# Tokens loaded already turned in a hybrid decoder block

## The reference

```
h = rmsnorm(x, norm_mix_w[l])            # x * rsqrt(mean(x*x) + eps) * w
proj = h @ w_in[l]
q, k, v, g, a_low, z, xbc, dt_raw = jnp.split(proj, split_pts, axis=-1)
... gla_out from q, k, v, g, a_low; ssd_out from z, xbc, dt_raw
x = x + concatenate([gla_out, ssd_out]) @ w_out[l]
h2 = rmsnorm(x, norm_ffn_w[l])
x = x + moe_ffn(h2, ...)                 # top 4 of 32 experts
return rmsnorm(x, final_norm_w)
```

## Time and profile before

| | us |
|---|---|
| median of 3 runs | 3452.66 (3452.18 to 3453.17) |
| the profiled execution | 3451.21 |
| its span on the core | 3449.3 |
| TensorE busy | 3383.7, 98% of the span |
| VectorE, ScalarE, GpSimd busy | 2166.1, 1612.5, 628.4 |
| one round (from round 2 on) | 124.9 |

### The profile page before, as it was taken

One profiled execution on the slowest core, in us unless ns is written; L12 is line 12 of the kernel. 1 busy time (PEld: TensorE's weight loads), 2 busy tenths in 40 slices (PEclk: granted clock), 3 DMA queues, 4 the chain that ended last, 5 costly groups with the idle time before them and its releaser, 6 DMA issues.

```text
span 3449.3 us, 56541 instructions
## 1 busy us (share of the span) xinstructions
PE 3383.7 (98%) x21127; PEld 3075.8 (89%) x21127; DVE 2166.1 (63%) x2796; ACT 1612.5 (47%) x2079; POOL 628.4 (18%) x840
## 2 busy tenths in 40 slices
PE   7999999999999999999999999999999999999997
PEld 6778888888888999999999999988888888888986
DVE  4565455445556555555566666577777777777777
ACT  4433333233333444444444444455555555555555
POOL 1011111111114111111121112121112212212213
PEclk9999999999999999999999999999999999999998
DMA  9888888897866555666566666567667767777878
GB/s 385 345 345 296 308 302 295 305 326 273 290 251 199 173 171 166 184 179 179 179 192 195 186 192 205 181 209 243 208 206 225 245 210 230 245 228 224 250 244 316
DMA packets 475311, 826.54 MB, mean 240 GB/s; under 512 B 21853, under 2 KB 419325, under 8 KB 458816
## 3 DMA queue, kind: packets, MB, share of 16 engines
q1 hardware_dynamic: 443392, 721.84, 60.0%
q0 software_dynamic: 24320, 75.95, 9.6%
q10 hardware_dynamic: 7488, 27.27, 2.2%
HBM read 726.16 MB, written 98.96 MB: 239 GB/s over the span
## 4 chain that ended last, share of the span: by engine, by line
PE 94%; DMA 2%; ACT 1%; DVE 1%; POOL 1%; issue 1%; SPq 0%; POOLq 0%; DVEq 0%; ACTq 0%
PE acc L2474 15%; PE pp L2069 13%; PE acc L2470 11%; PE acc L2471 10%; PE acc L2472 10%; PE acc L2476 7%; PE acc L2486 4%; PE acc L2488 4%; PE acc L2487 4%; PE pp L2058 3%; PE tpm L2443 2%; PE pp L2059 2%; PE tp L2035 1%; PE tpm L2449 1%; DMA uraw<-in_w_in 1%; PE seg L2170 1%
## 5 line engine op out<-in xcount | busy, mean ns | idle before, releaser
L1891 DVE TENSOR_TENSOR wlo<-raw,whi 128x2048 fp32r<-128x2048 f32 x384 | 875.9, 2288 | 302.4 <-ACT whi L1281 302.3
L1281 ACT ACTIVATE whi<-raw 128x2048 fp32r<-128x2048 f32 x384 | 730.1, 1910 | 152.6 <-PE acc L2488 102.3
L2474 PE MATMUL acc<-xhl,whi 128*128 128x512 f32 (+3 forms) x2304 | 763.8, 385 | 0.0
L690 POOL TENSOR_TENSOR gate_op<-gate_op 1x1 f32<-1x1 f32 x348 | 175.2, 504 | 2714.4 <-DVE ybuf L1929 526.2
L2476 PE MATMUL acc<-xhl,wlo 128*128 128x256 f32 (+3 forms) x2304 | 624.3, 271 | 0.0
L2470 PE MATMUL acc<-xhl,whi 128*128 128x272 f32 (+3 forms) x1792 | 534.9, 298 | 1.2 <-DVE xhl L1903 1.2
L2471 PE MATMUL acc<-xhl,whi 128*128 128x272 f32 (+3 forms) x1792 | 530.3, 296 | 0.0
L2472 PE MATMUL acc<-xhl,wlo 128*128 128x272 f32 (+3 forms) x1792 | 530.2, 296 | 0.0
L2474 PEld LDWEIGHTS acc<-xhl,whi 128*128 128x128 f32 x2304 | 432.0, 187 | 68.4
L1314 ACT ACTIVATE work<-acc,bgu 128x256 f32<-128x256 f32 (+7 forms) x400 | 173.1, 470 | 584.6 <-PE acc L2472 366.2
L2476 PEld LDWEIGHTS acc<-xhl,wlo 128*128 128x128 f32 x2304 | 437.3, 190 | 0.7
(11 more groups left out here) (336 smaller groups left out, 5369.3 us busy)
## 6 DMA issues: line engine op xcount, KB each, us to landing
u<-split_d SPq DMA_DIRECT2D x112, 2048.0 KB, 9.2
raw<-in_moe_w_gate SPq DMA_DIRECT2D x128, 1024.0 KB, 5.2
raw<-in_moe_w_up SPq DMA_DIRECT2D x128, 1024.0 KB, 5.3
raw<-in_moe_w_down SPq DMA_DIRECT2D x128, 1024.0 KB, 9.3
split_d<-u SPq DMA_DIRECT2D x16, 2048.0 KB, 13.0
uraw<-in_w_in SPq DMA_DIRECT2D x12, 1024.0 KB, 11.0
yT<-in_moe_b_down SPq DMA_DIRECT2D x18, 512.0 KB
xin<-in_x ACTq DMA_DIRECT2D x14, 512.0 KB, 9.8
```

Source lines behind the costliest of these rows:

```text
L690: pool.tensor_tensor(gate_op[0:1, 0:1], gate_op[0:1, 1:2], gate_op[0:1, 1:2], ALU.add).then_inc(gate_ran, 1)
L1281: act.activation(whi[:, q % RING, :, :], raw[:, q % RING, :, :], ACT.Copy).then_inc(a_hi, 1)
L1891: dve.tensor_tensor(wlo[:, q % RING, :, :], raw[:, q % RING, :, :], whi[:, q % RING, :, :].bitcast(F32), ALU.subtract).then_inc(v_lo, 1)
L2474: pe.matmul(into[:, 0:2 * n].rearrange("p (c n) -> p c n", c=2), hi_, of[:, k, :, 0:n], start=(k == 0), stop=False)
```

## The change

The host lays out x a second time as `x_turned`, with the features on the partitions: for each pair 128 partitions of 8 x 256 numbers, 8 KB in one run, as `hraw` wants them. In rounds 1 to 6 ScalarE issues one load of 1 MB of it into `hraw`, as the first thing of its body. The scaling pass is left out for tiles 4 to 15, and instead of eight transposes TensorE makes one, of the column of 128 roots read over and over (`roots_spread`): the result has the roots of the tokens along the free axis, the same on each partition. VectorE then multiplies the loaded rows by the norm's weight and by this (`turned_rows`, eight operations of 128x128). x is still loaded into `xin` as well, for the squares. GpSimd makes a root only after the transpose of the one before has read `st`, and the load into `xin` waits for the former square, no longer for the former transposes.

```diff
+        def done_twice(inst, first, second):
+            s, i = where[first]
+            turn[s] += 2
+            inst.then_inc(S[s], 2)
...
-            def norm_root(j, n):
+            def norm_root(j, n, turned=False):
                 after(pool, "act_norm.sq", j)
+                if turned:
+                    after(pool, "pe_tx.tx", j - 1)
...
             def x_in(j):
-                after(act, "pe_tx.tx", j - 2 if isinstance(j, int) and j == 2 else j - 1)
+                if isinstance(j, int) and j <= 4:
+                    after(act, "pe_tx.tx", j - 2 if j == 2 else j - 1)
+                else:
+                    after(act, "act_norm.sq", j - 1)
                 act.dma_start(xin[:, :], x[0, bass.ds(j * P, P), :]).then_inc(d_x, 16)
...
+                turned = not (isinstance(j, int) and j < 4)
+                if turned:
+                    after(act, "p_norm.rstd", j - 1)
+                c = act.activation(junk[:, :], src, ACT.Square, scale=1.0 / 32.0, accum_out=st[:, 0:1])
+                if turned:
+                    done_twice(c, "act_norm.sq", "act_norm.xn")
...
+                if tx and at >= 1:
+                    after(act, "dve_h.lo", s)
+                    act.dma_start(hraw[:, :, :], x_turned[bass.ds(s + 1, 1)].rearrange("one p k i -> (one p) k i")).then_inc(d_xt, 16)
                 if post:
...
-                if tx:
+                if tx and at == 0:
                     norm_xn(a + 3)
...
-                if more:
-                    norm_xn(a + 4)
...
+            def turned_rows(s, t):
+                after(dve, "pe_tx.tx", s * 2 + 2 + t)
+                dve.wait_ge(d_xt, s * 16)
+                for k in range(KD):
+                    rows = hraw[:, k, t * P:(t + 1) * P]
+                    c = dve.scalar_tensor_tensor(out=rows, in0=rows, scalar=nw[:, k:k + 1], in1=tp[:, 0:P],
+                                                 op0=ALU.mult, op1=ALU.mult)
+                done(c, "dve_hT.hT")
...
-                    h_rows(a + 2, 0)
+                    h_rows(a + 2, 0) if at == 0 else turned_rows(s, 0)
...
-                    h_rows(a + 3, 1)
+                    h_rows(a + 3, 1) if at == 0 else turned_rows(s, 1)
...
+            def roots_spread():
+                done(pe.transpose(tp[:, 0:P], st[:, 1:2].to_broadcast([P, P]), ident[:, :]), "pe_tx.tx")
...
-                    after(pe, "act_norm.xn", a + 2)
+                    after(pe, "act_norm.xn" if at == 0 else "p_norm.rstd", a + 2)
...
-                    transposes(8, lambda c: xin[:, c * P:(c + 1) * P], "pe_tx.tx")
+                    if at == 0:
+                        transposes(8, lambda c: xin[:, c * P:(c + 1) * P], "pe_tx.tx")
+                    else:
+                        roots_spread()
...
+    x_turned = _np.asarray(inputs["x"][0]).reshape(PAIRS, PW, KD, P).transpose(0, 3, 2, 1)
```

More of the change, by code:

```diff
@@ L141, with build @@
 PRIMED = UNITS
-def build(nc, x, columns, shared, moe_cols, w_in, gla_w_alpha_up, w_out, router_w, moe_w_gate, moe_w_up, moe_w_down, moe_b_down, final_norm_w, out):
+def build(nc, x, x_turned, columns, shared, moe_cols, w_in, gla_w_alpha_up, w_out, router_w, moe_w_gate, moe_w_up, moe_w_down, moe_b_down, final_norm_w, out):
     with ExitStack() as ctx:
@@ L323, in done @@
             inst.then_inc(S[s], 1)
+        def done_twice(inst, first, second):
+            s, i = where[first]
+            assert turn[s] % len(STEPS[s]) == i and where[second] == (s, i + 1), (first, turn[s])
+            turn[s] += 2
+            inst.then_inc(S[s], 2)
         def after(eng, step, n):
@@ L334, in build @@
         d_ru = [sem(f"d_ru{s}") for s in range(4)]
-        v_ws = sem("v_ws")
         a_uh, v_ul, pe_un = sem("a_uh"), sem("v_ul"), sem("pe_un")
         d_un, d_st = ([sem(f"{n}{s}") for s in range(4)] for n in ("d_un", "d_st"))
-        d_x, d_x1 = sem("d_x"), sem("d_x1")
+        d_x, d_x1, d_xt = sem("d_x"), sem("d_x1"), sem("d_xt")
         d_xres, d_x2, d_h2 = ([sem(f"{n}{t}") for t in range(2)] for n in ("d_xres", "d_x2", "d_h2"))
@@ L759, in body @@
                 if tx:
-                    norm_root(s * 2 + 3, n)
+                    norm_root(s * 2 + 3, n, at >= 1)
                     n = n + 1
@@ L771, in body @@
                 if more:
-                    norm_root(s * 2 + 4, n)
+                    norm_root(s * 2 + 4, n, True)
                     n = n + 1
@@ L971, in norm_sq @@
                 src = xres[:, 1, :] if second else xin[:, :]
-                done(act.activation(junk[:, :], src, ACT.Square, scale=1.0 / 32.0, accum_out=st[:, 0:1]), "act_norm.sq")
+                turned = not (isinstance(j, int) and j < 4)
[5 more added lines that the diff above has]
+                else:
+                    done(c, "act_norm.sq")
             def norm_xn(j):
@@ L1751, in small_weights @@
                 dve.wait_ge(d_wsm, 32)
-                dve.tensor_copy(wsr[:, :, 0:SMALL], wsm[:, :, :]).then_inc(v_ws, 1)
-                dve.wait_ge(v_ws, 1)
+                dve.tensor_copy(wsr[:, :, 0:SMALL], wsm[:, :, :]).then_inc(setup_v, 1)
+                dve.wait_ge(setup_v, DVE_SETUP + 1)
                 dve.tensor_tensor(wsr[:, :, 64:SROWS], wsm[:, :, :], wsr[:, :, 0:SMALL].bitcast(F32),
-                                  ALU.subtract).then_inc(v_ws, 1)
+                                  ALU.subtract).then_inc(setup_v, 1)
             h_rows(0, 0)
@@ L2094, in small @@
                 if isinstance(s, int) and s == 0:
-                    pe.wait_ge(v_ws, 2)
+                    pe.wait_ge(setup_v, DVE_SETUP + 2)
                 for k in range(KD):
@@ L2276, in body @@
                 if tx:
-                    after(pe, "act_norm.xn", a + 3)
+                    after(pe, "act_norm.xn" if at == 0 else "p_norm.rstd", a + 3)
                     if post:
@@ L2582, in _ @@
             chunk(i, SIZES[-1], True)
-_INS = ["x", "columns", "shared", "moe_cols", "w_in", "gla_w_alpha_up", "w_out", "router_w", "moe_w_gate",
+_INS = ["x", "x_turned", "columns", "shared", "moe_cols", "w_in", "gla_w_alpha_up", "w_out", "router_w", "moe_w_gate",
         "moe_w_up", "moe_w_down", "moe_b_down", "final_norm_w"]
@@ L2602 @@
     moe_cols = biases.reshape(E * 3 * KD, P).T
-    inputs = {**inputs, "columns": columns, "shared": shared, "moe_cols": moe_cols}
+    x_turned = _np.asarray(inputs["x"][0]).reshape(PAIRS, PW, KD, P).transpose(0, 3, 2, 1)
+    inputs = {**inputs, "x_turned": x_turned, "columns": columns, "shared": shared, "moe_cols": moe_cols}
     nc = _bacc.Bacc("TRN2", target_bir_lowering=False, num_devices=1)
```

## The result

The changed kernel took 3496.92 us (median of 4 runs, 3488.86 to 3499.49), the kernel before 3452.42 us on the same chip (4 runs). The ratio is 1.0123, 95% interval 1.0111 to 1.0135: slower by 1.2%, where 3456 us and a range up to 3470 were forecast. The profiled execution took 3488.86 us, so its trace shows 37.7 us of loss against the 3451.21 us of before's; the median has some 8 us more, on which see the last point of "Why the prediction was wrong".

The account below looks back on a forecast made before the run. The prediction took TensorE's own queue to bound the rounds touched. Terms -9.1 - 0.5 + 12.0 + 0.9 = +3.3 us on 3452.7 gave 3456 us, own range 3446 to 3460, wider range 3443 to 3470.

Parts of the forecast that it names:

- The transposes: TensorE, tiles 4 to 15: seven transposes fewer save 0.76 us a tile, 9.1 us for twelve tiles.
- VectorE's 2.15 us: VectorE: eight small products with a PSUM operand take 2.2 us a tile, 0.9 us more than the two before.
- the load's landing: `hraw` load: issued at 496.5, landed by 505.5; VectorE waits about a us, hurting only beyond 507.
- the place of the stall: TensorE idles 2 to 3 us before `x_piece(s, 2)`, put down to VectorE's xT sum.
- the delay D of the writes: ScalarE's queue: both xacc_d writes come later behind the 1 MB load, by 4.5 us, range 1 to 7.3.
- rival (b): Writes come much later: load gains nothing by its lead, delay 7.3 us, total 3470 us; chance 0.30 together with another rival.
- the slack formula: `x_piece(s, 2)` start less `h2_of` start less 2.45, less 0.76 for TensorE's earlier arrival; delay beyond this slack stalls TensorE.
- The estimate of 4.4 us for the load: DMA: skill's gpsimd-path fit, 2.0 us plus bytes over 436 GB/s; would mean no stall; the prediction doubted it.
- nothing is as near: VectorE, second tile of a round: longer products cost nothing, as the PSUM bank's next user stands far behind in TensorE's queue.
- stall before `x_piece(s, 2)`: TensorE, five rounds: waits of 2.1, 2.0, 2.9, 1.7 and 3.3 us from late writes, 12.0 us together.
- `decays` waits for `ssd_add`: TensorE, round 1: the late load delays products and `ssd_add` before `decays`; 0.9 us, bounds 0 and 5.
- round 0: ScalarE: dropping the scaling pass before a copy TensorE waited for gains 0.5 us, bounds 0 and 0.5.

Follow-up runs that it names:

- e8: Changed kernel with the load issued early, `ssd_add` ahead of `turned_rows`, and weight unit 3 of rounds 2 to 6 held until both writes landed: 3445.77 us, 0.9975 to before.
- e2: Changed kernel with the load issued from SyncE's queue, ahead of weight unit 3, instead of ScalarE's: 3485.19 us, 1.0081 to before.
- e6: Changed kernel with weight unit 3 of rounds 2 to 6 held on SyncE until both xacc_d writes have landed: 3460.06 us, 1.0014 to before.
- e5: The repaired kernel: changed kernel with the load issued early and `ssd_add` ahead of `turned_rows` for both tiles: 3449.54 us, 0.9986 to before.
- e1: Changed kernel with the load issued at the end of the round before, ahead of `ssd_squares(a)`: 3458.64 us, 1.0016 to before.
- e9: Kernel before the change, with only weight unit 3 of rounds 2 to 6 held until both writes have landed: 3453.09 us, 1.0002 to before.
- e3: Changed kernel with the load issued behind both xacc_d writes on ScalarE's queue: 3540.13 us, 1.0244 to before.
- e7: Changed kernel with 40 unused identity products on TensorE ahead of the transposes of `h2` in rounds 2 to 6: 3517.09 us, 1.0184 to before.
- e11: Changed kernel with 18 unused identity products on TensorE ahead of the transposes of `h2`, to fill the gap: 3488.50 us, 1.0101 to before.

## Why the prediction was wrong

**What held.** The transposes: a round of the repaired kernel lasts 123.43 us against 124.93, 1.50 less, where 2 x 0.76 = 1.52 was forecast; rounds 1 to 6 of e8 together last 8.7 us less than before, of the 9.1 forecast. The single transpose cost no more than its share: it takes 0.27 us from start to modelled end, but the round shortens in full. VectorE's 2.15 us, the load's landing before it was wanted in rounds 2 to 6, the place of the stall and what it would be put down to: all as written.

**The step that failed** is the delay D of the writes, "the two writes of 512 KB now queue behind 1 MB on the same queue". Its size was wrong, and so was what it was made of. The load did use its lead, as the prediction assumed against rival (b). But D was counted from the load's packets alone, as if both writes were late by the same and then kept the pace of the earlier trace rows. The first tile's `h2_of` was late by 1.9 to 2.3 us in rounds 3 to 5, the second's by 5.8 to 8.5. The second write's pace rested on something that I had not looked for: a pause of the weight queue 7 to 10 us into these rounds, in which q10 moved 0.52 MB in 3 us (round 4). The load takes the engines at the round's start, the weight unit issued there lands 13.4 us after its issue instead of 9.4, the next one follows it without a pause, and the second write runs beside that, packet by packet against 16 KB ones. To be behind the load on the queue isn't needed for the stall (e2), and without the weights beside the writes it doesn't make one (e6). What is open is why D was 4.4 and 7.8 us in rounds 2 and 6, where there was hardly a pause to lose, and why the write was late in e2, where the pause was there. The count of packets of the earlier trace rows was made over 6 us only, up to just before that pause. D came out at 6.7 us on average instead of 4.5, beyond the 5.2 from which rival (b) decides. The term measured 22.1 us where 12.0 was forecast; the slack formula gives with the measured Ds, less the slacks of 2.4, 2.5, 1.6, 2.8 and 1.2, the stalls 2.0, 6.0, 4.2, 4.1 and 6.6, together 22.9: that half of the step was right. The estimate of 4.4 us for the load, by the fit of the Trainium skill for the gpsimd path (DMA: Bandwidth & Descriptors, "Anatomy of one DMA — SWDGE (gpsimd) path"), didn't hold on this queue: the load took 7.4, and the second write, of half its size, 16.

**What had no term.** First the clock: all five stalls, of 1.88 to 6.43 us, were followed by work in part at the 1.2 GHz level, and `x_piece(s, 2)` took 9.2 us more in the five rounds. I priced a stall at its length. Then `ssd_add` behind `turned_rows`: I gave the second tile nothing ("nothing is as near") and found 0.53, 0.48, 0.85, 0.88, 0.85 and 0.63 us, 4.2 together; the first `decays` of round 1 waited 1.73 us where 0.9 was taken, since the load landed 8.2 us after its issue there and not 6. I had priced the products and not asked who waits for what stands behind them, for each tile; e5 shows the cure.

**The balance** of the profiled execution, over the span's 37.9 us (the measured size of the transposes is that of e8's rounds):

| term | forecast | measured |
|---|---|---|
| transposes | −9.1 | −9.0 (6 x 1.50) |
| stall before `x_piece(s, 2)` | +12.0 | +22.1 |
| slow clock in it | 0 | +9.2 |
| `decays` waits for `ssd_add` | +0.9 | +5.9 |
| round 0 | −0.5 | +1.1 |
| rest of rounds 1 to 6 | 0 | +4.5 |
| from round 7 on | 0 | +4.1 |

Of the rest, some 1.9 us go with the seven waits of `decays`: a round of e1 with 0.85 us of such a wait lasts 124.55 us, one of e5 without it 123.43, so that a wait costs 0.27 us beyond its length. The other 2.6 us, and what happens after round 6, I have not traced. Round 0 ended at 120.1 to 123.1 us in the profiled executions of all kernels here, so its 1.1 us say nothing on the 0.5 that was forecast. A round 7 lasts 200.7 to 200.9 us in the kernels without the load (before, e9) and 201.6 to 204.9 in those with it; the cause stays open, and so does why rounds 2 and 6 of e1 were still late.

**The median's 8 us more.** In the profiled executions of e3, e6, e7 and e11 round 1, which these edits don't touch ahead of its first `decays`, lasted 134.3 to 134.6 us, with 4.3 to 4.6 us of idle time before that `decays` and a slow stretch behind it: the load took 10.7 to 11.0 us to land. In the changed kernel's profiled execution it took 8.2, and the round 128.5. The profiled execution was the fastest of the changed kernel's four. So I take round 1 for the difference of 6 of those 8 us; a trace of a median execution of the changed kernel itself is not there.

## What to carry to other kernels

Before a transfer is added, look over the whole time in which the existing ones complete, not only where the new one is issued: a write that takes 10.5 us may owe much of its speed to a pause in another queue, and a megabyte ahead of it can close the pause. To put the load on another queue didn't help here (e2); what helped was to hold back the big transfer that isn't urgent (a wait of three lines on SyncE), or to issue the new one where nothing small is under way. Count all packets that stand ahead on the queue, not only those of the new transfer (e3). On an engine that bounds the kernel a stall can cost more than its length, as the work behind it may run at the lower clock: 9.2 us on top of 22.1 here; and when an operation ahead in a queue grows, ask at each of its places who waits for the one behind it.

## What the hardware showed that was not expected

- After 5.9 us of idle time in a stream of 98% busy TensorE, the granted clock was 0.50 for the next 6 us; stalls of 1.88 to 3.98 us too were followed by an `x_piece(s, 2)` 1.6 us longer. But with 1.92 us in e11 it was only 0.1 us longer, so a length of idle time doesn't alone decide it.
- The second 512 KB write of round 4 took 10.5 us from issue to the start of what waits for it before, and 16.3 us after; the same 1 MB load took 7.4 us ahead of the weights and 18.6 to 22.1 behind the writes (e3).
- In e2, 15 packets of ScalarE's queue, 0.05 MB, came in the 5 us after a stretch in which it had moved 0.48 MB in 3 us, and `h2_of` waited for the write until 20.4 us into the round: a transfer lands with its slowest packets, and the rate of its queue doesn't tell when.
- A product of f32 with 128 columns shows as two instructions of 0.11 us, a transpose of the same shape as one.
